# Four 512-token norms of a two-layer transformer kernel, taken in two token halves

## The reference

```
def rms_norm(x, gain):
    xf = x.astype(jnp.float32)
    y = xf * lax.rsqrt(jnp.mean(xf * xf, axis=-1, keepdims=True) + RMS_EPS)
    return (y * gain).astype(x.dtype)

def modulate(x, gain, shift, scale):
    return rms_norm(x, gain) * (1 + scale) + shift

def swiglu(h, w_in, w_out):
    a, b = jnp.split(h @ w_in, 2, axis=-1)
    return (jax.nn.silu(a) * b) @ w_out
```

## Time and profile before

| | |
|---|---|
| median of three runs | 2673.7 us |
| profiled execution | 2676.4 us |
| its span | 2674.6 us |
| mean granted TensorE clock | 0.973 |
| TensorE busy | 2545.5 us, 95% |
| VectorE busy | 1356.5 us, 51% |
| ScalarE busy | 1091.2 us, 41% |
| GpSimd busy | 247.1 us, 9% |

### The profile page before, as it was taken

The page is one execution under the profiler, slowest core; times in us unless marked ns, Lnnn a source line. Parts: engine busy times, 40 slices in busy tenths (PEclk is TensorE's granted clock), DMA queues, the critical chain, the costliest instruction groups (busy, mean ns, idle before and its releaser), DMA issues.

```text
span 2674.6 us, 45475 instructions
## 1 busy us (share of the span) xinstructions
PE 2545.5 (95%) x17855; PEld 1669.4 (62%) x17855; DVE 1356.5 (51%) x1911; ACT 1091.2 (41%) x1610; POOL 247.1 (9%) x235
## 2 busy tenths in 40 slices
PE   3899999999999999999999899999999999989999
PEld 3444444455644444444444568778888888777887
DVE  4755443453465553265532444365555654555664
ACT  5544423243354442254423321355444543444553
POOL 1810001004010000100003001021000010010001
PEclk7899999999999999999999899999999999999999
DMA  7976642330056673456643243238675764333574
GB/s 222 232 195 186 171 126 64 93 104 0 1 144 187 187 194 108 122 157 185 176 146 100 72 121 95 64 109 238 200 209 166 212 172 143 110 103 106 174 214 128
DMA packets 732734, 383.76 MB, mean 143 GB/s; under 512 B 12059, under 2 KB 729216, under 8 KB 732488
## 3 DMA queue, kind: packets, MB, share of 16 engines
q1 hardware_dynamic: 728312, 369.27, 49.2%
q0 software_dynamic: 3728, 10.98, 1.7%
q10 hardware_dynamic: 576, 1.83, 0.2%
HBM read 380.96 MB, written 1.08 MB: 143 GB/s over the span
## 4 chain that ended last, share of the span: by engine, by line
PE 87%; DVE 6%; DMA 3%; ACT 2%; issue 1%; POOL 0%; SPq 0%; ACTq 0%; DVEq 0%; POOLq 0%
PE PS L624 23%; PE PS L625 23%; PE PS L626 23%; DMA arena<-in_w_mod 2%; PE PS L735 2%; PE PS L643 1%; PE PS L642 1%; PE PS L641 1%; PE PS L761 1%; DVE WL L1362 1%; DVE arena L1518 1%; PE PS L909 1%; PE PS L601 1%; ACT WH L989 1%; PE PS L584 1%; PE PS L738 1%
## 5 line engine op out<-in xcount | busy, mean ns | idle before, releaser
L624 PE MATMUL PS<-XH,WH 128*128 128x256 f16 (+1 forms) x2912 | 948.6, 326 | 35.6 <-DVE XL L1524 21.0
L625 PE MATMUL PS<-XL,WH 128*128 128x256 f16 (+1 forms) x2912 | 948.1, 326 | 0.0
L626 PE MATMUL PS<-XH,WL 128*128 128x256 f16 (+1 forms) x2912 | 947.3, 325 | 0.0
L1362 DVE SCALAR_TENSOR_TENSOR WL<-W,WH 128x1024 f16<-128x1024 f32 (+1 forms) x520 | 666.0, 1319 | 287.1 <-ACT WH L989 287.0
L989 ACT ACTIVATE WH<-W 128x1024 f16<-128x1024 f32 (+1 forms) x520 | 551.2, 1107 | 611.7 <-PE PS L626 505.9
L624 PEld LDWEIGHTS PS<-XH,WH 128*128 128x128 f16 x2912 | 288.0, 99 | 224.5 <-issue 35.5
L626 PEld LDWEIGHTS PS<-XH,WL 128*128 128x128 f16 x2912 | 288.5, 99 | 181.8 <-issue 4.3
L625 PEld LDWEIGHTS PS<-XL,WH 128*128 128x128 f16 x2912 | 288.1, 99 | 171.3 <-issue 3.6
L624 PE MATMUL PS<-arena,WH 128*128 128x256 f16 (+1 forms) x1184 | 379.5, 321 | 0.8 <-DVE WL L1362 0.8
L625 PE MATMUL PS<-arena,WH 128*128 128x256 f16 (+1 forms) x1184 | 379.5, 321 | 0.0
L626 PE MATMUL PS<-arena,WL 128*128 128x256 f16 (+1 forms) x1184 | 379.4, 320 | 0.0
(11 more groups left out here) (232 smaller groups left out, 2317.1 us busy)
## 6 DMA issues: line engine op xcount, KB each, us to landing
arena<-in_w_mod SPq DMA_DIRECT2D x144, 512.0 KB, 6.8
W<-in_ffn_a_in SPq DMA_DIRECT2D x88, 512.0 KB, 4.9
W<-in_ffn_b_in SPq DMA_DIRECT2D x88, 512.0 KB, 4.8
W<-in_w_ffn_gu SPq DMA_DIRECT2D x88, 512.0 KB, 4.2
W<-in_ret_in SPq DMA_DIRECT2D x48, 512.0 KB, 4.4
W<-in_ffn_a_out SPq DMA_DIRECT2D x32, 704.0 KB, 5.6
W<-in_ffn_b_out SPq DMA_DIRECT2D x32, 704.0 KB, 5.7
W<-in_w_ffn_down SPq DMA_DIRECT2D x32, 704.0 KB, 5.6
```

The costliest lines, as they stand in the source:

```text
L624: mm(dst, wh, xh, start=(kp == 0 and c == 0), stop=False, skip_group_check=True)
L625: mm(dst, wh, xl, start=False, stop=False, skip_group_check=True)
L626: return mm(dst, wl, xh, start=False, stop=(kp == g["parts"] - 1 and c == kc - 1), skip_group_check=True)
L1362: stt(WL[:, k, t, 0:g["kc"], :], W32[:, k, t, 0:g["kc"], :], W_SCALE, WH[:, k, t, 0:g["kc"], :], ALU.mult, ALU.subtract).then_inc(lo_ready, 1)
```

## The change

The norms 1 to 4 are taken in two halves of 256 tokens. The last two blocks of the resid GEMM ahead are computed by halves (in an ffn the last four: those of kp = 0 do both halves one behind the other): first half of the next-to-last block, first half of the last, then the second halves. Within the second halves TensorE does the sums and the spread of half 0. In even_u, ffn_0b_in and ffn_1a_in, which have 512 tokens, the first two blocks run as first half of block 0, the sums of half 1, first half of block 1 with the spread of half 1 in it, then both second halves. ret_q, with 256 tokens, runs block 0 on half 0, the sums of half 1, block 1, the spread of half 1.

```
+                def half_three(k, kp, pair, t, c, s):
+                    H = T // 2
+                    xh, xl = g["rhs"](kp, c, T, kc)
+                    xh, xl = xh[:, H * s:H * s + H], xl[:, H * s:H * s + H]
+                    wh, wl = WH[:, k, t, c, :], WL[:, k, t, c, :]
+                    dst = PS[:, 2 * pair + s, H * t:H * t + H]
...
+                    kp = g["parts"] - 1
+                    half_block(nb - 2, 2, kp, 1, (1, kc // 2), lambda: pe_half_sums(n, 0)).then_inc(block_used, 1)
+                    half_block(nb - 1, 3, kp, 1, (0, kc // 2), lambda: pe_half_spread(n, 0)).then_inc(block_used, 1)
+
+                def split_head():
+                    n = g["norm"]
+                    for s in range(2):
+                        for b in range(2):
+                            if s == 0:
+                                pe.wait_ge(units_drained, g["u0"] + b - 1)
+                                pe.wait_ge(lo_ready, 2 * (g["w0"] + b) + 2)
+                            for c in range(kc):
+                                if b == 0:
+                                    pe.wait_ge(xl_ready, H0[n] + DC * s + c + 1)
+                                for t in range(2):
+                                    ins = half_three(b, 0, b, t, c, s)
+                                if (s, b, c) == (0, 1, kc // 2):
+                                    pe_half_spread(n, 1)
+                            if s == 1:
+                                ins.then_inc(block_used, 1)
+                                if g["mods"]:
+                                    pe_mod(g["m0"] + b, b)
+                            elif b == 0:
+                                pe_half_sums(n, 1)
...
+                        if first and NORMS[g["norm"]]["halved"]:
+                            (pe_half_sums if b == 0 else pe_half_spread)(g["norm"], 1)
```

On ScalarE the end of a resid GEMM becomes:

```
+                act.activation(warm[:, 1:2], mats[:, 1, 0:1], ACT.Sqrt)
+                squares(n, range(2 * done, 4))
+                half_squares(0, 2)
+                half_squares(0, 3)
+                half_root(0)
+                begin(after, (0,))
+                half_squares(1, 2)
+                half_apply(0, range(0, 4))
+                half_squares(1, 3)
+                begin(after, (1,))
+                half_apply(0, range(4, DC))
+                half_root(1)
+                act.activation(warm[:, 0:1], mats[:, 1, 0:1], ACT.Silu)
+                half_apply(1, range(DC))
+                begin_mods(after)
```

and on VectorE (half_add adds two pieces to X, half_h scales one, half_low makes one XL):

```
+                dve.wait_ge(half_used, 2 * g["r"] + 1)
+                half_add(0, 2)
+                dve.wait_ge(half_used, 2 * g["r"] + 2)
+                half_add(0, 3)
+                half_inverse(0)
+                dve.wait_ge(block_used, g["w0"] + nb - 1)
+                half_add(1, 2)
+                split(after, 0, 0)
+                dve.wait_ge(rstd_ready, M0[n] + 1)
+                for c in range(DC + 1):
+                    if c < DC:
+                        half_h(0, c)
+                    if c >= 1:
+                        half_low(0, c - 1)
+                    if c == 3:
+                        dve.wait_ge(block_used, g["w0"] + nb)
+                        half_add(1, 3)
+                        split(after, 0, 1, (0,))
+                    if c == 5:
+                        split(after, 0, 1, (1,))
+                half_inverse(1)
+                dve.wait_ge(rstd_ready, M0[n] + 2)
...
```

More of the change, by code:

```diff
@@ L302, in program @@
         GEMMS = []
+        SPLIT_TAIL = ("ffn_0a_out", "even_out", "ffn_0b_out", "ffn_1a_out")
         def gemm(name, kind, w, kc, blocks, T, cols, rhs, parts=1, tok=False, dest=None, scale=1.0, gate=None, ffn=None, need=(), need_2=None, norm=None):
             g = dict(name=name, kind=kind, w=w, kc=kc, blocks=blocks, T=T, cols=cols, rhs=rhs, parts=parts, tok=tok,
-                     dest=dest, scale=scale, gate=gate, ffn=ffn, units=blocks // parts, need=list(need), need_2=need_2, norm=norm, mods=0, m0=0, packed=name == "ret_g")
+                     dest=dest, scale=scale, gate=gate, ffn=ffn, split_tail=name in SPLIT_TAIL, split_head=False, units=blocks // parts, need=list(need), need_2=need_2, norm=norm, mods=0, m0=0, packed=name == "ret_g")
             last = GEMMS[-1] if GEMMS else None
@@ L311, in gemm @@
             if kind == "resid":
-                g["r"] = sum(x["kind"] == "resid" for x in GEMMS)
-                g["then"] = (1, 2, 3, 4, 5, 6, 7, 9, 10, 11)[g["r"]]
+                r = sum(x["kind"] == "resid" for x in GEMMS)
+                g["then"] = (1, 2, 3, 4, 5, 6, 7, 9, 10, 11)[r]
+                g["r"] = sum(x["kind"] == "resid" and x["split_tail"] == g["split_tail"] for x in GEMMS)
                 g["order"] = [(u, kp) for v in (0, 2) for kp in range(parts) for u in (v, v + 1)]
@@ L385, in drained, with halves @@
             return g["u0"] + g["units"]
+        for g, after in zip(GEMMS, GEMMS[1:]):
+            if g["split_tail"]:
+                after["split_head"] = after["T"] == g["T"]
+        def halves(T):
+            return [(s, s if T == BOTH else 0, slice(s * T // 2, (s + 1) * T // 2)) for s in range(2)]
         def segs(T):
@@ L685, in pe_gemm @@
                 n, mods, begin = g["units"] // 2, g["mods"], 0
-                if g["norm"] is not None:
+                if g["split_head"]:
+                    split_head()
+                    begin = 1
+                elif g["norm"] is not None:
                     turn_of(0, mods > 0, True)
@@ L825, in _ @@
             pe_gemm(gi["ffn_0a_in"])
-            pe_gemm(gi["ffn_0a_out"], {b: lambda b=b: filter_step(b) for b in range(5)} | {7: lambda: pe.wait_ge(filt_ready, 5)})
+            pe_gemm(gi["ffn_0a_out"], {b: lambda b=b: filter_step(b) for b in range(5)} | {5: lambda: pe.wait_ge(filt_ready, 5)})
             pe_gemm(gi["even_u"])
@@ L1070, in act_resid @@
                     split(g, b // 2, b % 2)
-                    while g["done"][done] <= b - 2:
+                    while done < (2 if g["split_tail"] else 4) and g["done"][done] <= b - 2:
                         squares(n, (2 * done, 2 * done + 1))
@@ L1075, in act_resid @@
                         between[b]()
+                if g["split_tail"]:
+                    act_split_tail(g, after, done)
+                    return
                 act.activation(warm[:, 1:2], mats[:, 1, 0:1], ACT.Sqrt)
@@ L1414, in rest, with store @@
                     tt(GL[:, j, 0:T], ffn_g[:, k:k + 1, 0:T], GH[:, j, 0:T], ALU.subtract).then_inc(gl_done, 1)
-                def store(i, k):
+                def store(i, k, halved=False):
                     dve.wait_ge(block_used, w0 + k + 1 + 2 * i)
+                    if halved:
+                        for t in range(2):
+                            src = PS[:, 2 * k:2 * k + 2, T // 2 * t:T // 2 * t + T // 2]
+                            dst = g["dest"][:, 4 * i + 2 * k + t, 0:T].rearrange("p (s t) -> p s t", s=2)
+                            ins = ts(dst, src, g["scale"] / W_SCALE, None, ALU.mult)
+                        ins.then_inc(units_drained, 1)
+                        return
                     if g["tok"]:
@@ L1458, in dve_gemm @@
                 else:
-                    if n > 1:
-                        with dve.Fori(1, n) as i:
+                    if g["split_head"]:
+                        for k in range(2):
+                            store(0, k, True)
+                            split(g, 1, k)
+                    if n > at:
+                        with dve.Fori(at, n) as i:
                             for k in range(2):
@@ L1480, in dve_resid @@
                 u = 0
+                if g["split_tail"]:
+                    for b in range(2, nb):
+                        while u < 2 and g["done"][u] <= b - 2:
+                            dve.wait_ge(block_used, g["w0"] + g["done"][u] + 1)
+                            add(u).then_inc(units_drained, 1)
+                            u += 1
+                        split(g, b // 2, b % 2)
+                        if b in between:
+                            between[b]()
+                    for u in range(u, 2):
+                        dve.wait_ge(block_used, g["w0"] + g["done"][u] + 1)
+                        add(u).then_inc(units_drained, 1)
+                    dve_split_tail(g, after)
+                    return
                 for b in range(2, nb + 1):
```

216 lines of the change are left out of this document (181 added, 35 removed).

## The result

| | before | changed |
|---|---|---|
| median of five runs | 2674.2 us | 2687.3 us (2683.6 to 2689.5) |
| profiled execution, its span | 2676.4, 2674.6 us | 2689.5, 2687.7 us |
| mean granted TensorE clock | 0.973 | 0.973 |

The changed kernel is slower: ratio 1.0048, 95% interval 1.0033 to 1.0062, 13.1 us by the medians. 2688 was forecast.

A forecast was written before the change was run, and what follows sets the result against it. PE was busy 2545.5 of 2674.6 us; four norms cost 49 us. Changes of +1.0, +2.2, +2.5, +4.0 and 0.5 for POOL gave +10.2; clock added 2.0 and 2.0: +14.2, forecast 2688 us, 8-in-10 range 2677 to 2698.

The forecast's parts named there:

- two f32 sets: In each halved norm, two sets of f32 sums and spread hold PE, 3.2 us a set, 6.4 us per norm.
- stall before c = 3: In each head's first-half block 0, PE waits 2.7 us for the fourth chunk's low part, behind a DVE weight split.
- stall before c = 5: In each head's first-half block 0, the second weight split, behind c = 4, costs PE another 1.3 us.
- w_mod waits: Behind even_out and ffn_0b_out, PE waits 1.0 and 0.7 us for w_mod weight splits, +1.4 us in each.
- wait ahead of ret_q's third block: In ret_q, half 1's norm, store and split precede block 2, which starts 8.8 us after the spread.
- clock behind the first stall: In each head, half clock after the first stall costs 0 to 1.75 us; 0.5 taken, 2.0 in four.
- clock in ret_q's block 2 and 3: After ret_q's 8.8 us of idle PE, unpaced work at half clock loses 1.0 to 3.3 us; 2.0 taken.
- POOL: Behind even_out, two weight splits meet POOL's adds of half 1: 0 to 1.1 us, 0.5 taken.
- rival C: Clock falls at each first stall and stays low 8.0 us, slowing sums and block 1's first half; 2700 us, 11%.
- The cost of before: The four norms' cost to PE before the change: 10.9, 11.0, 16.0 and 10.9 us, 48.8 in all.
- A: Norms hidden: half 0's low parts ready as PE asks and ret_q's block 2 not waiting; 2658 us, 8%.
- B: ret_q does not wait, since block 2's weights are loaded long before; no change, 2677 us, 11%.

The follow-up runs named there:

- order in half 0: Changed kernel with block 1's weight conversion (ACT) and split (DVE) placed behind all of half 0, in all four norms; 2671.7 us, ratio 0.9996.
- three norms repaired: Changed kernel with ffn_1a_out whole as before; in the other three norms, block 1's conversion and split behind half 0, w_mod products behind block 1's second half; 2660.3 us.
- the spread moved: Changed kernel with one line moved: PE runs the spread of half 1 inside ret_q's block 1 instead of behind it; 2682.3 us, ratio 1.0044.
- all four repairs: Changed kernel with block 1's conversion and split behind half 0, w_mod products behind block 1's second half, spread inside ret_q's block 1, block 2's entries before half 1's norm; 2656.0 us.

## Why the prediction was right

The order of DVE and ACT, the wait in ret_q and the price of the f32 sets were the forecast's mechanism, and the experiments above confirm each. The norms were forecast to cost 63.0 us and cost 65.2; the time was forecast at 2688 and is 2687.3. The terms one by one:

| term, us | taken | behind even_out | behind ffn_1a_out |
|---|---|---|---|
| two f32 sets | 6.4 | 5.6 | 5.6 |
| stall before c = 3 | 2.7 | 3.0 | 2.45 |
| stall before c = 5 | 1.3 | 0.46 | 0.92 |
| w_mod waits | 1.0 and 0.7 | 0.86 and 0.58 | none |
| wait ahead of ret_q's third block | 8.8 | none | 8.85 |
| clock behind the first stall | 0.5 | 0.55 | 2.5 |
| clock in ret_q's block 2 and 3 | 2.0 | none | 2.1 |

**Stalls.** The mechanism, its place and its size were as worked out from durations of before: the split amid half 0 that hangs on the tail's end. Both stalls together make PE 4.2 us late behind ffn_0b_out, where the clock stayed at 1.00, and 4.8 behind even_out; 4.2 and 4.3 were forecast, and 0.5 behind even_out for POOL, whose part no run tests. The second stall was forecast at 1 to 1.5 us and is that only behind ffn_0b_out (1.09 us): at the lower clock PE takes longer to reach it, and it shrinks to 0.46 to 0.92. Removing that order removes the stalls, but for 0.7 us behind even_out. The ret_q wait is the sum of queue entries that it was said to be, since moving the spread takes off 3.6 us and moving the entries takes off the rest.

**f32 sets** were 0.4 us too dear each, 3.2 in all, and just under the low end that I gave (2.9). I had read them from a 256-token norm at 0.13 us a piece, two pieces to a matmul; 24 pieces in a row start every 0.112 (2.68 from 758.02 to 760.70). They still are the reason why halving can't win more: 5.6 of the 7.8 us that remain.

**Clock.** This is the term that was mis-sized. The forecast said that what follows a first stall is paced by DVE and costs 0.5. From the end of the first stall to the f32 sums the same matmuls took 4.83 us behind ffn_0b_out, at 1.00; 5.38 behind even_out; 6.52 behind ffn_0a_out and behind ffn_1a_out. There the low stretch also reached into the f32 sums, which took 2.62 and 2.73 us for 1.96; nothing paces the sums. So the clock cost 0.55 us behind even_out, where most of the slow work came off the second stall and the short pauses before later chunks, and 2.35 and 2.5 us behind the two others. Behind ffn_0b_out it fell after the w_mod waits, where nothing paces PE, and cost 1.7. Low stretches lasted 3.4 us behind even_out and ffn_0b_out and 6.8 behind the others, up to twice the 3.5 that I took from the earlier trace rows, but not the 8.0 of rival C. (Those 8.0 were parts of two stretches of 6.8 us each, from 1510.5 and from 1520.7; the window of the earlier trace rows ends in the second.)

The Trainium skill (TensorE: Matmul & The Clock Gate, Terms) prices a throttled stretch at half its length, which I set aside as too high. Behind ffn_0b_out's w_mod waits this trace agrees (1.7 for 3.4 us); behind ffn_1a_out it has 2.5 for 6.8 us, of which 0.9 fell on the second stall, and behind even_out 0.55 for 3.4.

**What cancelled.** The sets are 3.2 us below the forecast, the clock in the four heads is 7.1 us for the 2.0 taken, and all else together is within 0.3 of it: that makes the 2.2 by which the norms' cost was missed. The cost of before was forecast 1.0 short (48.8 for 49.8), and the rest of the program gave back 2.8 in the profiled run, by no merit of the forecast. So that the profiled time is forecast within about 1 us (2690.6 for 2689.5) is in part luck; without those 2.8 the forecast would have been 2 us low by the profile. By the medians, +13.1 against +14.2 forecast, it was 1 us high.

**Rivals.** A said that it decides if the stall at c = 3 is under 1 us. It wasn't, so A failed here, for the reason given. With that stall at 0.74 or gone and ret_q's order mended, the kernel lands at 2656, near A's 2658: A was a right description of another order. That the figures agree so well is partly luck, since A counts the sets 0.4 us too dear and 2.8 us of w_mod waits, which that kernel does not have. B failed: the wait was there, though the weights were loaded. C failed: the clock fell behind the first stall in three heads of four and stayed low for 3.4 to 6.8 us.

## What to carry over

To hide a serial step behind halves, write down for the engine that feeds TensorE every entry of its queue between the first input and the last, and look for the one that hangs on the end of what you wanted to overlap; here one weight split in such a place cost more than the whole overlap won, and moving it (and, at the narrower GEMM, work that the next matmul does not read) turned +13 us into -17. A halved norm pays its f32 matmuls twice, 2.8 us a set, so what it can win is the old cost less 5.6. Count a stall together with the slow matmuls that may follow it: 2.5 to 3 us of waiting brought nothing more in one head and 0.55 to 2.5 us in the three others.

## What was not expected of the hardware

- The same instructions from the rotary products to the end took between 1087.3 and 1090.3 us in twelve profiles (before, changed and ten experiments), 1087.3 in the changed kernel's. The low clock lay at other places of the short norms, or for longer or shorter, in most of them; three that took 1090.1 (before, order in half 0, three norms repaired) have it at the same places. The scatter is more than half of the 5.3 us that I took for no change.
- The same idle time did not always bring the lower clock. In the changed kernel it fell behind idle times of 2.45 us in two heads and of 3.04 in a third, and not behind 2.45 us in the fourth; in the profile with the spread moved it did not fall behind ffn_0a_out's 2.45 us either (1.00 from 461 to 470). Two w_mod waits of 0.9 and 0.6 us were followed by it behind ffn_0b_out in the changed kernel, and not behind even_out. It stayed at 1.00 with waits of 0.7 and 2.0 us (all four repairs). In ret_q it was low from 1540.4, 2.9 us into a wait of 8.85, and stayed low for 4.3 us of work.
- An f32 matmul of 64 columns stands in the trace as two rows, and such rows follow each other every 0.112 us, about as far apart as f16 matmuls of 256 columns (0.109). So one f32 matmul of 64 columns takes about as long as two f16 ones of 256.
